# GpSimd takes the low parts of twelve gate panels from DVE in a fused two-block network kernel

## The reference, cut to what matters

```python
for i in range(DEPTH):                       # DEPTH = 2
    proj = rmsnorm(h, norm_g[i]) @ w_in[i]   # 1024 x 4376
    (hq, hf, hi, hgo, hz, nq, kcm, vcm, ksl, vsl, kwn, vwn, ngate, nz) = split(proj)
    o_hg = hgrn2_chunkwise(...)              # gated linear recurrence, 4 heads
    y_hg = rmsnorm(o_hg) * sigmoid(hgo) * silu(hz)
    o_nsa = gates * (compressed, selected and window attention)   # 8 heads
    y_nsa = o_nsa * silu(nz)
    h = h + concat([y_hg, y_nsa]) @ w_out[i]
    h = h + sigmoid(rmsnorm(h) @ w_pg[i]) * (p[i] @ w_pp[i])
```

## Time and profile before

| | |
|---|---|
| median of 3 runs | 1141.74 us |
| the profiled execution's own time | 1140.99 us |
| its span, first to last instruction | 1139.2 us |
| TensorE clock granted, mean | 0.972 |
| PE busy | 1053.7 us, 92% |
| DVE busy | 716.9 us, 63% |
| ACT busy | 601.2 us, 53% |
| POOL busy | 5.0 us, all at the start |

### The profile page before, as it was taken

How to read it: one execution, slowest core, us unless ns; L and a number is a source line. 1 busy time by engine, 2 the same in 40 slices (tenths; PEclk the granted TensorE clock), 3 DMA queues, 4 the chain that set the end, 5 groups by cost and what they waited for, 6 DMA issues and landing times.

```text
span 1139.2 us, 21429 instructions
## 1 busy us (share of the span) xinstructions
PE 1053.7 (92%) x9017; PEld 993.2 (87%) x9017; DVE 716.9 (63%) x1080; ACT 601.2 (53%) x876; POOL 5.0 (0%) x13
## 2 busy tenths in 40 slices
PE   5999787999998887999999999999899899999997
PEld 5998766899995876998999999999878799999996
DVE  6746556567557365578667767666754559666574
ACT  5543565466535554476646545445644456545543
POOL 1000000000000000000000000000000000000000
PEclk9999899999999999999999999999988899999999
DMA  8553512254646121275444655555363235555531
GB/s 281 158 144 113 158 63 75 75 168 129 190 116 200 60 75 38 80 253 157 149 150 147 212 180 178 183 180 167 104 205 99 75 111 185 185 184 184 184 111 38
DMA packets 144748, 163.59 MB, mean 144 GB/s; under 512 B 6072, under 2 KB 135552, under 8 KB 144672
## 3 DMA queue, kind: packets, MB, share of 16 engines
q1 hardware_dynamic: 143752, 161.04, 44.2%
q10 hardware_dynamic: 632, 1.30, 0.3%
q0 software_dynamic: 288, 0.14, 0.1%
HBM read 161.43 MB, written 1.05 MB: 143 GB/s over the span
## 4 chain that ended last, share of the span: by engine, by line
PE 68%; DVE 14%; ACT 11%; issue 4%; DMA 2%; SPq 1%; DVEq 0%; ACTq 0%
PE ps L440 20%; PE ps L441 19%; PE ps L442 19%; DVE panels_low L1682 4%; ACT panels_high L1163 4%; ACT probs L1149 2%; PE ps L458 2%; PE ps L530 1%; DMA panels<-in_w_in 1%; DVE neg_max L1705 1%; DVE squares L1646 1%; DVE probs L1721 1%; PE ps L661 1%; ACT unscaled L1149 1%; PE ps L568 1%
## 5 line engine op out<-in xcount | busy, mean ns | idle before, releaser
L1682 DVE TENSOR_TENSOR panels_low<-panels,panels_high 128x2048 fp32r<-128x2048 f32 (+1 forms) x146 | 329.8, 2264 | 273.6 <-ACT panels_high L1163 273.5
L440 PE MATMUL ps<-input_high,panels_low 128*128 128x256 f32 x1600 | 464.9, 291 | 28.9 <-DVE input_low L1677 7.8
L441 PE MATMUL ps<-input_low,panels_high 128*128 128x256 f32 x1600 | 457.3, 286 | 0.0
L442 PE MATMUL ps<-input_high,panels_high 128*128 128x256 f32 x1600 | 457.0, 286 | 0.0
L1163 ACT CAST panels_high<-panels 128x2048 fp32r<-128x2048 f32 (+1 forms) x146 | 274.2, 1881 | 143.3 <-PE ps L442 116.9
L440 PEld LDWEIGHTS ps<-input_high,panels_low 128*128 128x128 f32 x1600 | 311.4, 195 | 35.1 <-issue 14.5
L441 PEld LDWEIGHTS ps<-input_low,panels_high 128*128 128x128 f32 x1600 | 311.8, 195 | 0.3
L442 PEld LDWEIGHTS ps<-input_high,panels_high 128*128 128x128 f32 x1600 | 311.5, 195 | 0.0
L440 PE MATMUL ps<-ffn_hidden_high,panels_low 128*128 128x256 f32 x352 | 99.5, 283 | 6.6 <-DVE ffn_hidden_low L2208 3.8
L441 PE MATMUL ps<-ffn_hidden_low,panels_high 128*128 128x256 f32 x352 | 99.5, 283 | 0.0
L442 PE MATMUL ps<-ffn_hidden_high,panels_high 128*128 128x256 f32 x352 | 99.4, 282 | 0.0
(11 more groups left out here) (284 smaller groups left out, 1329.5 us busy)
## 6 DMA issues: line engine op xcount, KB each, us to landing
panels<-in_ffn_up SPq DMA_DIRECT2D x44, 1024.0 KB, 5.1
panels<-in_w_in SPq DMA_DIRECT2D x32, 1024.0 KB, 5.8
panels<-in_ffn_down SPq DMA_DIRECT2D x22, 1024.0 KB, 4.9
panels<-in_mix_w_in SPq DMA_DIRECT2D x20, 1024.0 KB, 5.4
panels<-in_w_out SPq DMA_DIRECT2D x8, 1024.0 KB, 5.2
panels<-in_w_pg SPq DMA_DIRECT2D x8, 1024.0 KB, 5.3
panels<-in_mix_w_out SPq DMA_DIRECT2D x8, 1024.0 KB, 6.9
panels<-in_w_pp SPq DMA_DIRECT2D x2, 1024.0 KB, 4.8
```

Source lines behind the costliest of these rows:

```text
L440: pe.matmul(dst, w[1], x[0], start=start, stop=False if not kw else True, **kw)
L441: pe.matmul(dst, w[0], x[1], start=False, stop=False if not kw else True, **kw)
L442: return pe.matmul(dst, w[0], x[0], start=False, stop=stop, **kw)
L1682: V.tensor_tensor(low_slots[slot][:, 0:size], raw[n % SLOTS][:, 0:size], high_slots[slot][:, 0:size].bitcast(F32), ALU.subtract).then_inc( ...
```

## The change

The low parts of hgo0, hgo1, hz0, hz1, nz0 and nz1 in both layers (12 of 146) are made by POOL, which waits for the same `high_ready` count and adds one to a semaphore of its own. PE and SP wait for that one where the panel is one of these. `low_ready` now counts only DVE's low parts, so the numbers that are waited for are taken from a new table, `LOW_NO`.

```diff
+POOL_KEYS = [k for k in SPLIT_KEYS if k[0] in ("hgo0", "hgo1", "hz0", "hz1", "nz0", "nz1")]
+POOL_NO = {k: i for i, k in enumerate(POOL_KEYS)}
+LOW_NO = {k: i for i, k in enumerate(k for k in SPLIT_KEYS if k not in POOL_NO)}
...
+        def low_is_ready(eng, key):
+            if key in POOL_NO:
+                eng.wait_ge(pool_low_ready, POOL_NO[key] + 1)
+            else:
+                eng.wait_ge(low_ready, LOW_NO[key] + 1)
...
             def split(key):
-                pe.wait_ge(low_ready, SPLIT_NO[key] + 1)
+                low_is_ready(pe, key)
...
             # in split_low, DVE
-                    low_part(n, q % SLOTS, q + 1, panel_size(n))
+                    if SPLIT_KEYS[q] not in POOL_NO:
+                        low_part(n, q % SLOTS, q + 1, panel_size(n))
                     next_low[0] += 1
...
         @block.gpsimd
+            for key in POOL_KEYS:
+                q, n = SPLIT_NO[key], LOAD_NO[key]
+                pool.wait_ge(high_ready, q + 1)
+                nc.gpsimd.tensor_tensor(low_slots[q % SLOTS], raw[n % SLOTS], high_slots[q % SLOTS].bitcast(F32),
+                                        ALU.subtract).then_inc(pool_low_ready, 1)
...
             # in slot_empty, SP
-                        sp.wait_ge(low_ready, SPLIT_NO[key] + 1)
+                        low_is_ready(sp, key)
```

More of the change, by code:

```diff
@@ L173, in build @@
         high_ready, low_ready = sem("panel_high_ready"), sem("panel_low_ready")
+        pool_low_ready = sem("panel_low_ready_by_pool")
         panel_free = {}
+        def low_is_ready(eng, key):
[3 more added lines that the diff above has]
+                eng.wait_ge(low_ready, LOW_NO[key] + 1)
         order_of = {}
@@ L1053, in _ @@
                 ffn_base[l] = up0 = [bank_fills[b] for b in range(4)]
-                q0 = SPLIT_NO[("gate", l, 0)]
+                q0, low0 = SPLIT_NO[("gate", l, 0)], LOW_NO[("gate", l, 0)]
                 def up(par, i, normed=None):
@@ L1060, in up @@
                         pe.wait_ge(psum_free[b], i + up0[b])
-                        pe.wait_ge(low_ready, i * 6 + (q0 + 3 * par + half))
+                        pe.wait_ge(low_ready, i * 6 + (low0 + 3 * par + half))
                         slot = (q0 + FFN_SLOT[half]) % SLOTS
@@ L1073, in down @@
                         slot = (q0 + 2 + 3 * (FF_ROUNDS - 1)) % SLOTS
-                        pe.wait_ge(low_ready, q0 + 3 * FF_ROUNDS)
+                        pe.wait_ge(low_ready, low0 + 3 * FF_ROUNDS)
                     else:
-                        pe.wait_ge(low_ready, i * 6 + (q0 + 3 * par + 5))
+                        pe.wait_ge(low_ready, i * 6 + (low0 + 3 * par + 5))
                     pe.wait_ge(act_ready, 2 * i + (par + 1 + FF_ROUNDS * l))
@@ L2272, in ffn @@
             def ffn(l):
-                n0, q0 = LOAD_NO[("gate", l, 0)], SPLIT_NO[("gate", l, 0)]
+                n0, low0 = LOAD_NO[("gate", l, 0)], LOW_NO[("gate", l, 0)]
                 def round_loads(par, i):
@@ L2278, in round_loads @@
                         n = n0 + 3 * par + 2 + kind
-                        sp.wait_ge(low_ready, 6 * i + (q0 + 3 * par + kind))
+                        sp.wait_ge(low_ready, 6 * i + (low0 + 3 * par + kind))
                         if kind < 2:
```

## The result

The changed kernel takes 1145.39 us (median of 20 runs, 1143.73 to 1148.3); the kernel before, beside it on the same chips, 1142.71 (20 runs, 1140.63 to 1145.24). The ratio is 1.0029, 95% interval 1.0022 to 1.0035: 2.7 us or 0.29% slower. The difference is small, but the interval leaves 1 out, so the kernel is slower. The prediction was 1135.5 us, 6.2 us faster.

The account below looks back on a forecast made before the run. PE was taken as the bound. Gains of 1.1 us at the levels and 2.0 in the attention made 3.1 a layer, 6.2 in both; from 1140.99 that gives 1134.8, with 0.75 for the median 1135.5 (range 1121 to 1147).

Parts of the forecast that it names:

- What bounds the kernel: PE, busy 1053.7 of 1139.2 us, sets the end; work off DVE is worth only what PE stops waiting.
- POOL's 4.6 us an instruction: Each low part on POOL takes twice DVE's 2.29 us, its two inputs being taken one after the other.
- hgo0 and nz0 as worth nothing: Moving these two low parts gains nothing, since PE does not wait near them.
- The view that the engines exclude each other: A POOL instruction and a DVE instruction with two SBUF inputs cannot run together; the main case rests on it.
- the level after them, wanted at 118.8, waits until hz0 is done at 123.3: Last level before hgo1's chunk: held once, then 0.75 us; PE starts at 125.2, not 126.29, gaining 1.1 a layer.
- the hidden layer's four instructions: On DVE, before the last level: taken as not held by POOL, so they go at 117.3.
- a gain of 1.1 each: Levels of each layer: PE starts hgo1's chunk at 125.2 in place of 126.29.
- The lower clock: PE's slow rows after its waits at the levels, 1.5 us a layer; expected to stay under exclusion.
- The attention: First normalise no longer waits behind nz1's low part; PE's waits of 1.08 and 1.43 shrink: 2.0 us a layer gained.
- the 3.8: PE's wait of 3.80 us at 188.07 in the attention, behind wo1's low part: none of it gained.
- B: At the levels POOL gets between two DVE instructions: 2.4 us a layer, 4.8 in all slower, 1146.5; chance 0.22.
- A: The engines do not hinder each other: both waits at the levels vanish, 17.6 us gained in all, 1124; chance 0.26.

Follow-up runs that it names:

- e4_pieces: The changed kernel with each of POOL's twelve instructions cut into eight of 128x256: 1123.91 us, ratio 0.9849 to the kernel before.
- e5_hidden: The changed kernel with the hidden layer's add moved to ACT and its copy replaced by a product reading PSUM: 1142.86 us, ratio 1.0009 to the kernel before.
- e1_row: The changed kernel with POOL making only hgo1, hz0 and hz1, DVE the other three again: 1149.8 us, ratio 1.0066 to the kernel before.
- e2_rest: The changed kernel with POOL making only hgo0, nz0 and nz1, DVE the other three again: 1137.44 us, ratio 0.9961 to the kernel before.
- e3_none: The changed kernel with POOL's twelve instructions left out, PE and SP waiting for the high part: 1121.46 us, ratio 0.9821 to the kernel before.
- e11_att: The kernel before with only nz1, wo0 and wo1 put behind the second, fourth and sixth unit's row maxima in DVE's queue: 1125.99 us, ratio 0.9858.

## Why the prediction was wrong, point by point

- **What bounds the kernel** held: PE, and only what it waits for. POOL's 4.6 us an instruction held (4601 ns), and so did hgo0 and nz0 as worth nothing: hgo0's does hold an instruction of DVE, but PE isn't waiting there. One reading was wrong without costing anything: not every panel of this stage has landed long before it is needed. ACT waits 5.38 and 1.12 us for the weights of hgo1 and hz0 before the change (it begins their high parts at 112.16 and 115.18), and 4.85 and 1.35 after it (at 111.81 and 115.06), so SP's loads did not come later.
- **The view that the engines exclude each other** held (e4_pieces against the change: 21.5 us for the length of POOL's instructions alone). Two steps that were built on it failed.
- **The step that cost most** is "the level after them, wanted at 118.8, waits until hz0 is done at 123.3. It takes 0.75 us". The overlap was priced with one hold by POOL, as if the level's second product and all behind it then ran free. With the next low part ready, POOL gets in between the two products. e5_hidden shows this step by itself: with the hidden layer free, both products of the level were held in layer 1, by hz0 and by hz1 (4.46 and 4.71), and PE waited 8.80 us in one piece. In layer 2 POOL's instructions fell on the next level's products (3.68 and 4.71), and PE waited 0.51 and 4.97. All in all the kernel was 0.95 us slower than before (0.5 faster to 2.6 slower by its interval), where the prediction had 6.2 faster. By the medians that is 7.2 of the 8.9 us between the predicted and the measured difference (6.2 faster, 2.7 slower).
- **The other step** is "the hidden layer's four instructions (one tile or PSUM each, mostly) still go at 117.3"; freeing them gives the other 1.7 us (e5_hidden against the change). One SBUF tile as input isn't enough to be free: the TENSOR_SCALAR and the COPY, from SBUF to SBUF, were held 4.50 and 3.60 us; PSUM as an input and the RECIPROCAL went free. The Trainium skill, SBUF — State Buffer (SBUF: two separate sides) names two kinds of DVE instruction that contend with GpSimd, one with two SBUF inputs and one in a two-port mode. The same page (Who interferes with whom) counts copy, cast and tensor_scalar to those that can enter such a mode. The trace agrees with both kinds (4.50 and 3.60 us here, 4.82 for the product of forget_key); the prediction took only the first. Which of POOL's three meets the two varies: hz0 and hz1 in layer 1, hgo1 and hz0 in layer 2 and in e1_row (1.90 and 3.61 us, 1.66 and 3.62).
- **The size of the loss.** The levels cost 5.3 and 3.4 us where I had a gain of 1.1 each. PE's waits grew by 8.38 + 0.51 - 2.98 - 2.75 = 3.2 us in layer 1. The lower clock, which I had let stay as it was, is most of the rest: between the two waits PE's small products take 2.1 us in place of 1.3, all 24 rows of the chunk and not some 17 lie 0.21 us apart, and the products behind it are slower too. The stretch from 92 to 142 us shows it, before and after (busy time and count of PE, PEld, DVE, ACT, POOL, then the granted clock):

```profile
92.00:142.00 50.00, 44.27 (x446) 37.89 (x443) 27.54 (x49) 24.47 (x37) 0.00 (x0) 0.93 0.44 137
```

```profile
92.00:142.00 50.00, 41.11 (x424) 34.64 (x410) 32.99 (x44) 21.79 (x34) 18.38 (x4) 0.86 0.43 135
```

- **The attention** was right in its mechanism and about its size: 2.0 a layer predicted, 2.1 and 1.2 in the two profiled executions, and 2.6 a layer by the medians of e2_rest, where it is the only gain. The waits of 1.08 and 1.43 us are gone (0.58 is left in layer 2) and the 3.8 stays.
- **The rivals.** B was what happened: one chain of DVE held by two POOL instructions after the other, 8.4 + 0.5 us of waiting in layer 1 where B said 9. It named L1833 and L1834 as the two; in layer 1 they were the hidden layer's, and in e5_hidden they are L1833 and L1834 themselves. Its total, 4.8 us slower, is above the measured 2.7, because layer 2 lost less and, in the profiled pair, the second block came out 1.5 us shorter. That its 1146.5 lies only 1.1 from 1145.39 is in part luck: it starts from 1141.74, where the kernel before took 1142.71 beside the change. I gave B 0.22, with the hidden layer outside the lock; e5_hidden shows that B's course doesn't need the hidden layer, only that POOL has its next low part ready (ACT had made hz1's high part by 120.3). A's condition did not hold, and its size was low: without POOL's instructions it is 21.2 us (e3_none), not 17.6. The terms of before were too small: moving hz0 and hz1 in DVE's queue gives 7.4 a layer where I had 5.0 + 1.5 = 6.5.
- **Left open**: why the levels of layer 2 cost 1.9 less than those of layer 1. Its rows show the course of e1_row, with hz1 holding a product of the level (4.40), and PE's waits there (4.08 and 3.74 us, where they were 2.50 and 2.84) grew by 2.5 and not 3.2; no run isolates it. In the profile of e11_att the first mark is at 144.8 and not at 142.3. Of this, 1.7 us are weights that landed later: ACT begins hgo1's high part at 113.84 after 7.18 us of waiting for the DMA, before it was at 112.16 after 5.38. Why they landed later isn't shown. The 16.4 us are the difference of the medians of all runs and do not rest on that profile.

## What to carry to other kernels

Before work goes from DVE to GpSimd, count the DVE instructions between SBUF tiles that stand on the path while GpSimd works: each may wait for a whole GpSimd instruction. Several long ones in a row were the worst case here. With pieces of 128x256 the same move was 18.8 us faster than the kernel before, with whole panels 2.7 slower. And ask first whether the engine or only the place in its queue is at fault: putting five low parts a layer behind the short work they stood ahead of, on the same engine, gave 32 us. In a profile a held instruction looks busy, so look for one whose duration has changed.

## What the runs showed of the hardware that was not expected

- Beside GpSimd's TENSOR_TENSOR these DVE instructions, all in float32, were held up to its end: TENSOR_TENSOR with two SBUF inputs even at 128x16 (4.53 us at 95.94 in the change), TENSOR_SCALAR 128x64 and COPY 128x128 from SBUF to SBUF. These were not: RECIPROCAL 128x64 in SBUF (0.56), COPY from PSUM (0.41 at 123.12 in e1_row), TENSOR_TENSOR with one input in PSUM (0.22, and 0.28 in e5_hidden).
- Where both engines had work ready, they mostly took turns instruction by instruction: three whole instructions of GpSimd held three of DVE's, six halves held five. In layer 2 of e5_hidden two products of DVE went through in a row, and GpSimd's instruction lasted 5385 ns in place of 4514.
- A piece of 128x256 takes GpSimd 775 ns on the mean, a half 2427 and a whole 128x2048 4601, and consecutive ones overlap by a few hundredths of a us. By busy time, eight pieces cost 29% more (71.0 us for 55.1) and two halves 4.5% (57.6).
